# The first four gate blocks of a Fourier mixer computed from rows that are not yet normalised, and a reordered last head before them

## The reference

```python
def rms_norm(x, g):
    var = jnp.mean(xf * xf, axis=-1, keepdims=True)
    return (xf * lax.rsqrt(var + EPS)) * g

# layer 1, after x = x + gate * (y @ w_out)
h = rms_norm(x, norm_g[1]) * (1.0 + sc) + sh
def fourier_mixer(h, w_in, w_out):
    u, z = jnp.split(h @ w_in, 2, axis=-1)      # 2048 features each
    y = jnp.fft.fft2(ug, axes=(1, 3), norm='ortho').real
    return (y * jax.nn.silu(z)) @ w_out
```

## Time and profile before

| what | us |
|---|---|
| median of three executions | 2534.68 |
| the profiled execution's own time | 2534.45 |
| its span | 2532.8 |
| TensorE (PE) busy | 2466.3 |
| VectorE (DVE) busy | 1632.1 |
| ScalarE (ACT) busy | 993.6 |
| mean granted TensorE clock, as a share of full speed | 0.989 |

### The profile page before, as it was taken

The page is one execution under the profiler, slowest core; times in us unless marked ns, Lnnn a source line. Parts: engine busy times, 40 slices in busy tenths (PEclk is TensorE's granted clock), DMA queues, the critical chain, the costliest instruction groups (busy, mean ns, idle before and its releaser), DMA issues.

```text
span 2532.8 us, 40390 instructions
## 1 busy us (share of the span) xinstructions
PE 2466.3 (97%) x14398; PEld 2151.2 (85%) x14398; DVE 1632.1 (64%) x2378; ACT 993.6 (39%) x1338; POOL 118.1 (5%) x138
## 2 busy tenths in 40 slices
PE   7999999999999998999999999989999999999998
PEld 3888888888888876888889999989999878888886
DVE  7577777777777765445555343468999985534446
ACT  4345444444444423333345222234555543322223
POOL 0011111121111100000000000000000000000000
PEclk9999999999999998999999999999999999999999
DMA  6212222222212222222222222222232222222223
GB/s 242 80 58 76 81 66 66 69 71 75 74 58 75 100 84 75 83 84 75 87 89 91 86 88 91 91 92 89 93 99 99 92 85 99 91 99 91 93 98 100
DMA packets 61983, 223.90 MB, mean 88 GB/s; under 512 B 6736, under 2 KB 8784, under 8 KB 61552
## 3 DMA queue, kind: packets, MB, share of 16 engines
q1 hardware_dynamic: 58992, 211.08, 25.1%
q0 software_dynamic: 2944, 12.19, 1.4%
HBM read 221.15 MB, written 2.10 MB: 88 GB/s over the span
## 4 chain that ended last, share of the span: by engine, by line
PE 92%; DVE 4%; ACT 1%; issue 1%; DMA 1%; ACTq 0%; DVEq 0%; SPq 0%
PE ps L489 81%; PE ps L662 4%; PE ps L684 1%; PE ps L546 1%; PE ps L675 1%; DMA ada_raw<-in_ada_weights_dram 1%; DVE w_lo L1593 1%; PE ps L694 1%; PE ps L695 1%; ACT w_hi L1050 1%; PE ps L696 1%; PE ps L703 1%; PE ps L649 1%; DVE n_tmp L1617 0%; PE ps L632 0%
## 5 line engine op out<-in xcount | busy, mean ns | idle before, releaser
L1050 ACT ACTIVATE w_hi<-w_raw 128x1024 fp32r<-128x1024 f32 (+1 forms) x360 | 377.8, 1050 | 935.7 <-PE ps L489 925.9
L1593 DVE TENSOR_TENSOR w_lo<-w_raw,w_hi 128x1024 fp32r<-128x1024 f32 (+1 forms) x360 | 435.3, 1209 | 226.4 <-ACT w_hi L1050 224.3
L489 PE MATMUL ps<-n_hi,w_hi 128*128 128x512 f32 (+1 forms) x992 | 320.3, 354 | 12.2 <-DVE n_lo L1620 8.5
L489 PE MATMUL ps<-n_lo,w_hi 128*128 128x512 f32 (+1 forms) x992 | 319.4, 354 | 0.0
L489 PE MATMUL ps<-n_hi,w_lo 128*128 128x512 f32 (+1 forms) x992 | 318.0, 352 | 0.0
L489 PE MATMUL ps<-h_hi,w_hi 128*128 128x512 f32 x640 | 266.6, 417 | 4.3 <-DVE h_lo L1725 2.6
L489 PE MATMUL ps<-h_hi,w_lo 128*128 128x512 f32 x640 | 251.8, 393 | 0.0
L489 PE MATMUL ps<-h_lo,w_hi 128*128 128x512 f32 x640 | 251.0, 392 | 0.0
L489 PEld LDWEIGHTS ps<-n_hi,w_hi 128*128 128x128 f32 x992 | 174.5, 189 | 45.6 <-issue 10.8
L489 PEld LDWEIGHTS ps<-n_lo,w_hi 128*128 128x128 f32 x992 | 174.3, 189 | 26.1 <-issue 0.2
L489 PEld LDWEIGHTS ps<-n_hi,w_lo 128*128 128x128 f32 x992 | 174.5, 189 | 25.8
(11 more groups left out here) (367 smaller groups left out, 4969.1 us busy)
## 6 DMA issues: line engine op xcount, KB each, us to landing
w_raw<-in_weights_dram SPq DMA_DIRECT2D x376, 512.0 KB, 3.3
ada_raw<-in_ada_weights_dram SPq DMA_DIRECT2D x4, 2048.0 KB, 20.9
gate_raw<-in_gate_weights_dram POOLq DMA_DIRECT2D x16, 512.0 KB, 3.6
x<-in_x_dram SPq DMA_DIRECT2D x1, 2048.0 KB, 12.6
x<-in_x_dram POOLq DMA_DIRECT2D x1, 2048.0 KB, 8.0
out_dram<-fin SPq DMA_DIRECT2D x16, 128.0 KB, 1.9
xc<-in_ctx_dram SPq DMA_DIRECT2D x1, 1024.0 KB, 19.3
masks<-in_masks_dram POOLq DMA_DIRECT2D x1, 512.0 KB, 5.1
```

Source lines behind the costliest of these rows:

```text
L489: last = nc.tensor.matmul(o, w, xp, start=start and n == 0, stop=stop and n == 2)
L1050: run(w_hi[:, s, 0:n], w_raw[:, s, 0:n], ACT.Copy).then_inc(hi_ready[s], 1)
L1593: tt(w_lo[:, s, 0:n], w_raw[:, s, 0:n], w_hi[:, s, 0:n].bitcast(F32), ALU.subtract).then_inc(lo_ready[s], 1)
```

## The change

**In the last head.** TensorE's part k of the output projection (k under 4) waits only for the accumulator that was last read from its own bank. On VectorE `passed(2)` stands directly behind `passed(1)`, and `early_after(6)` stands behind the whole norm of head 15's output; on ScalarE the root comes ahead of `early_after(6)`. The zeroing of the sums, the gain `scale[:, 2]` and twice the shift move up here as well.

**On the residual's rows.** As soon as a row of `x` is added, ScalarE writes `g_hi` = x times gain, rounded, and VectorE writes `g_lo`, its remainder (`raw_row`, `raw_row_lo`). TensorE waits for one early row instead of three. The loop over rows 4 to 7 is written out.

**The gates.** Gate blocks 0 to 3 (`RAW`) multiply these rows (`raw_gate`), with the mean for the norm placed inside the first. Beside each of the 8 triples stand two matmuls of 2 columns with the same weights and the shift (`shift_hl`: hi and lo). VectorE multiplies each result by the rate and adds up the shift's part (`raw_gate_scaled`), ScalarE applies the Silu with that as its bias (`raw_gate_row`). The normalised rows are made between these steps (`normal_tmp`, `normal_hi`, `normal_lo`), since the other 12 gate blocks and the transform still use them. Only gate block 4 is woven with their arrival. The remaining 11 blocks are spread as one beside each of rows 0 to 4 of the transform and two beside each of rows 5 to 7.

```diff
@@ pe_head, begin_output
-                        pe.wait_ge(acc_free, HEADS * 6 + 2)
+                        if k < EARLY:
+                            pe.wait_ge(acc_free, HEADS * 6 - 1 + k)
@@ TensorE, rows 4 to 7 and the gates
-            residual(RC, (KD - EARLY) // 2, 2, whole(y_hi, y_lo), T, done=EARLY)
-            mean(N1, T, n1["sum"][:, 0])
+            for i in range((KD - EARLY) // 2):
+                st.enter(0, 4)
+                for a in range(2):
+                    for q in range(2):
+                        s = take(a * 2 + q)
+                        if q == 0:
+                            pe.wait_ge(RC["res"], (3, 5, 7, 8)[i * 2 + a])
...
+            def raw_gate(n):
+                s = take(n % 2)
+                if n == 0:
+                    pe.wait_ge(RC["res"], KD + 1)
+                if n > 1:
+                    pe.wait_ge(z_scaled, n - 1)
+                side = ps[:, (4, 3, 5, 7)[n], 0:2]
+                for k in range(KD):
+                    if n == 0:
+                        if k == KD - 2:
+                            mean(N1, T, n1["sum"][:, 0])
+                        pe.wait_ge(raw_lo, k + 1)
+                    c = slice(k * P, (k + 1) * P)
+                    done = tiles(s, [ps[:, n % 2]], whole(g_hi, g_lo), [k], k == 0, k == KD - 1, k)
...
+                    nc.tensor.matmul(side, w_hi[:, s, c], shift_hl[:, k], start=k == 0, stop=False)
+                    done = nc.tensor.matmul(side, w_lo[:, s, c], shift_hl[:, k], start=False, stop=k == KD - 1)
...
+            s = take(0)
+            pe.wait_ge(z_out, RAW + 1)
+            tiles(s, [ps[:, 0]], as_cut(N1, whole(nf_hi, nf_lo)), range(KD), True, True).then_inc(w_used[s], 1)
+            turn(0)
+            gates_of(RAW // 2, 1)
+            over_tokens(0)
@@ ScalarE, rows
+            def raw_row(m_):
+                act.wait_ge(RC["res"], m_ + 3)
+                run(g_hi[:, m_], x1[:, m_], ACT.Identity, bias=zero[:], scale=scale[:, 2, m_:m_ + 1]).then_inc(raw_hi, 1)
+                act.wait_ge(RC["add"], m_ + 2)
+                run(n1["sq"][:, 0], x1[:, m_], ACT.Square).then_inc(RC["sq"], 1)
             for k in range(EARLY):
-                square_one(RC, k, x1[:, k], n1["sq"][:, 0], 2)
+                raw_row(k)
@@ ScalarE, normalised rows
+            after(0); raw_gate_row(0); normal_hi(0); after(1); raw_gate_row(1); normal_hi(1); normal_hi(2)
+            after(0); raw_gate_row(2); normal_hi(3) ... normal_hi(6); after(1); raw_gate_row(3); normal_hi(7)
@@ VectorE, last head
                 passed(1)
+                if i is None:
+                    mine(10)
+                    passed(2)
                 cut_output()
                 take_z()
                 early_after(5)
-                mine(10)
-                passed(2)
-                early_after(6)
@@ VectorE, early rows
+            def early_row(k):
+                dve.wait_ge(early_done, k + 1)
+                stt(x1[:, k], ps[:, k], gates[:, k, 0:1], x1[:, k], ALU.mult, ALU.add).then_inc(RC["res"], 1)
+                raw_row_lo(k)
+                add_square(RC, k, *sums)
+            early_row(0); early_row(1); after(2 * EARLY - 1); early_row(2); early_row(3)
@@ VectorE, gates and normalised rows
+            def raw_gate_scaled(n):
+                side = ps[:, (4, 3, 5, 7)[n]]
+                st.wait_done(dve, n % 2)
+                own.mark(v.tensor_copy(z_part[:, n:n + 1], side[:, 0:1]))
+                tt(z_rows[:, n], ps[:, n % 2], rate, ALU.mult)
+                own.wait()
+                tt(z_shift[:, n:n + 1], z_part[:, n:n + 1], side[:, 1:2], ALU.add).then_inc(z_scaled, 1)
+            after(0); raw_gate_scaled(0); normal_tmp(0); normal_tmp(1); normal_lo(0)
+            after(1); raw_gate_scaled(1); normal_lo(1); normal_tmp(2); normal_tmp(3); normal_lo(2)
+            after(0); raw_gate_scaled(2); normal_lo(3)
+            for k in range(4, KD - 1):
+                normal_tmp(k)
+                normal_lo(k)
+            after(1); raw_gate_scaled(3); normal_tmp(KD - 1); normal_lo(KD - 1)
```

More of the change, by code:

```diff
@@ L54 @@
 EARLY = 4
+RAW = 4
 Z_BANK = 2
@@ L326, in program @@
         N0, N0C, N1, NMIX = [norm_sems(t, "sum", "mean", "root", "tmp", "hi", "lo") for t in ("n0", "n0c", "n1", "nmix")]
[L327 to L328 removed]
+        NFIN, NOUT = norm_sems("nfin", "mean", "root"), norm_sems("nout", "sum", "mean", "root", "lo")
+        NF1, NF2 = [norm_sems(t, "mean", "root", "hi", "lo") for t in ("nf1", "nf2")]
         R0, R0C, RC, RF, RD1, RM, RD2 = [
@@ new lines, in _ @@
+            for i in range(RAW // 2):
+                st.enter(0, 2)
+                raw_gate(2 * i)
+                raw_gate(2 * i + 1)
+                st.leave(1)
+            st.enter(0, 2)
+            s = take(0)
[4 more added lines that the diff above has]
+            over_tokens(0)
+            st.leave(1)
+            with hinted(pe, 0, 2) as a:
+                st.enter(a, 2)
+                turn(a * 2 + 1)
+                gates_of(a + 3, 0)
+                over_tokens(a * 2 + 1)
+                turn(a * 2 + 2)
+                gates_of(a + 3, 1)
+                over_tokens(a * 2 + 2)
@@ L810, in pe_group @@
+            st.leave(2)
+            with hinted(pe, 0, 3) as b:
+                st.enter(b, 2)
+                turn(b + 5)
+                gates_of(b + 5, 0)
+                over_tokens(b + 5)
+                gates_of(b + 5, 1)
+            st.leave(3)
             def pe_group(i, j):
@@ new lines, in _, with normal_tmp, normal_lo @@
+            rate = n1["sq"][:, 0]
+            dve.wait_ge(N1["root"], 1)
+            own.link(v.reciprocal(rate, rate))
+            def normal_tmp(k):
+                if k > 1:
+                    dve.wait_ge(N1["lo"], k - 1)
+                stt(n1["tmp"][:, k % 2], x1[:, k], scale[:, 2, k:k + 1], rate, ALU.mult, ALU.mult
+                    ).then_inc(N1["tmp"], 1)
+            def normal_lo(k):
+                dve.wait_ge(N1["hi"], k + 1)
+                stt(nf_lo[:, k], n1["tmp"][:, k % 2], ada1[:, k, 0:1], nf_hi[:, k].bitcast(F32), ALU.add, ALU.subtract
+                    ).then_inc(N1["lo"], 1)
@@ new lines, in _ @@
+            normal_tmp(1)
+            normal_lo(0)
+            after(1)
+            raw_gate_scaled(1)
+            normal_lo(1)
+            normal_tmp(2)
+            normal_tmp(3)
+            normal_lo(2)
+            st.leave(1)
+            st.enter(0, 2)
+            after(0)
+            raw_gate_scaled(2)
+            normal_lo(3)
+            for k in range(4, KD - 1):
+                normal_tmp(k)
+                normal_lo(k)
+            after(1)
+            raw_gate_scaled(3)
@@ L1984, in fold @@
+            normal_tmp(KD - 1)
+            normal_lo(KD - 1)
+            st.leave(1)
             def fold(c, later=0):
@@ L2014, in frequencies_lo @@
                 tt(lo[:, 0:HALF_T + 1], p_cos[:], hi[:, 0:HALF_T + 1], ALU.subtract).then_inc(dve_ft, 1)
+            fold(0)
+            for n in range(2):
+                own.link(v.memset(middle[:, n:HALF_T + 1:2], (-1) ** n / T ** 0.5))
             st.enter(0, 2)
             after(0)
-            fold(0)
+            turned_lo(0)
+            fold(0, 1)
             dve.wait_ge(dft_split["act"], 1)
```

214 lines of the change are left out of this document (133 added, 81 removed).

## The result

| | median us | runs | lowest to highest |
|---|---|---|---|
| before, same chip | 2534.18 | 20 | 2531.92 to 2537.18 |
| after | 2537.62 | 20 | 2535.61 to 2541.32 |

The ratio is 1.0015, with a 95% interval of 1.0009 to 1.0022: 3.4 us slower. Forecast were 2525.0 and a range up to 2533. The profiled execution after took 2541.32 us, its span is 2539.6. It is the longest of the 20, 3.7 us above their median, so what the change costs in all is read from the medians; the trace serves for places and durations.

The account below looks back on a forecast made before the run. TensorE, 92% of the span, was taken as the bound, so gains come only from its waits and low clock. The last head's entry gave 4.1 us, the later steps 5.6, in all 9.7: 2525.0 us, range 2521 to 2533.

Parts of the forecast that it names:

- Memory adds nothing: In the sum: each slot's load follows its split as before, DMA share of the transform 0.26, so no time added.
- the clock: Rival, raw gates: tiny matmuls lower TensorE's clock, a block takes 12 us instead of 7.15; 2539.5 us, chance 0.08.
- A: Entering the last head: the counter wait causes TensorE's gap at 868.83 to 871.41; removing it saves 4.1 us.
- Fetch: Rival: the gap at 871.41 is instruction fetch at a loop exit, so nothing is saved there; 2529.1 us, chance 0.25.
- B: Last head's states: two updates move up from 918.11, the 2.2 us wait and low clock go; lead 4.0 us.
- D: First output block needs the first early row, not the third: no wait; lead 7.5, then 9.2 us after two blocks.
- C: Last head's norm: root earlier, reciprocal no longer behind block 8's split; y_lo at 929.2 instead of 934.0, lead 4.8 us.
- E: Output rows: raw rows take 2.9 us each, so block 10 waits 3.3 us plus 1.5 low clock; lead falls to 4.4.
- F: Gates ahead of the norm: two-column matmuls cost 0.11 us apiece, 7.15 a block; late normalised rows put the fold at 1021.3.
- G: Transform: 11 blocks instead of 14 remain, 75.4 us, no wait; stretch ends at 1097.3 instead of 1102.9.
- the dear pairs: Rival: two-column matmuls cost 0.25 us each, 6.7 us later; 2531.7 us, chance 0.14 shared with late blocks 11, 13, 15.

Follow-up runs that it names:

- after256: The changed kernel with 160 unused bytes behind shift2, so all later tiles lie 256 bytes above their place before: 2525.01 us (0.9967).
- acc_only: The kernel before with only TensorE's counter waits of the early blocks taken one by one: 2529.93 us (0.9984).
- lasthead: The kernel before with those counter waits one by one, passed(2) moved up on VectorE and the root ahead of early_after(6) on ScalarE: 2526.59 us (0.9971).
- supply: The kernel before with 56 more two-column matmuls behind the mean of N1, where TensorE waits for the norm: 2547.03 us (1.0052).
- fewside256: The changed kernel with tiles 256 bytes up, leaving out 28 of the 32 pairs of two-column matmuls: 2524.76 us (0.9964).

## Why the prediction was wrong

**The failed step is a term that the sum did not have.** The unit in it, "one takes 0.228 and a block of 24 takes 5.45 us", was taken from before and held fixed. The sentence "Memory adds nothing" in the sum spoke of the loads of weights; of the tiles' places nothing was said. The diff showed the two tiles taken ahead of `z_rows`; the prediction did not ask what they push. That term measures 12.1 to 12.6 us (after256 against the changed kernel), more than the whole forecast gain, and turned its sign; the range missed by 4.6 us. No rival had it. The one on the slower side was the clock; its 2539.5 lies near the measured 2537.6 by chance, for in the raw gates of the changed kernel the clock stayed up (the stretch's view):

```profile
984.00:1009.00 25.00, 25.00 (x134) 20.89 (x133) 16.12 (x21) 10.97 (x14) 0.00 (x0) 1.00 0.20 64
```

**The rest of the sum held until the transform.** In after256, where the unit holds, the last loop head's norm stands 0.6 us later than before (868.34 against 867.71), which I add to the leads:

| place | forecast lead, A included | after256 |
|---|---|---|
| kept rows, 934.05 before | 4.1 + 4.8 = 8.9 | 8.0 + 0.6 = 8.6 |
| end of the output rows, 984.84 | 4.1 + 4.4 = 8.5 | 7.65 + 0.6 = 8.3 |
| first transposes, forecast 1021.3 - 4.1 | at 1017.2 | 1018.1 - 0.6 = 1017.5 |
| first products behind the transform, 1119.10 | 9.7 | 6.0 + 0.6 = 6.6 |

- **A** was right in cause and size: 3.7 us by the medians, 4.1 in the trace (acc_only starts 1.2 later and is 3.0 ahead at the first products behind the transform), forecast 4.1. The Fetch rival was wrong for 871. For 1445 it was right that a gap may go where no wait was changed; its cause is not shown.
- **B to D** were right together: in after256 no wait on `states` is left, the reciprocal stands right behind the root, block 8 starts unwaited at 928.91 (11.2 us ahead with the 0.6, forecast 11.6), and TensorE wants block 10 at 942.86 - 2.88 - 0.6 = 939.4, forecast 942.95 - 4.1 = 938.9. lasthead against acc_only prices B and ScalarE's half of C: 3.3 us by medians, 4.7 in the trace (1116.14 to 1111.42 at the first products behind the transform). D has no run of its own.
- **E** was right in place and nearly in size, 2.6 to 2.9 for 3.3 us, but it bought less than it seemed: moved away, it returns at block 11, so the cover of 0.9 us a block was too thin for one more row.
- **F** was right in the unit. A triple with its pair took 0.93 us in the changed kernel (984.71 to 985.64), 0.91 in after256, forecast 0.9. The rule of the Trainium skill, "TensorE: Matmul & The Clock Gate", section "Back-to-back issue gap", some 25 ns for a matmul of 1 to 64 columns, does not fit: 0.233 us for two (0.913 less three times 0.227). The same section gives that figure for an isolated matmul and says that it counts too little where weights are loaded between small ones, as they are here. Of the waits forecast at 0.9, 3.9 and 0.5 the first two came, with 0.5 and 3.4.
- **G** failed by some 3 us: "so no wait". Two things were missed. The low clock behind the 3.4 us wait lasts into the first block of the transform (from 1018.13 it is 7.5 us to the first products with `F_hi`, before 6.0; the clock is 0.80 from 1018.1 to 1026), where I had allowed 0.6. And TensorE waits 1.3 for `t_lo`, because ScalarE stands still 2.5 us in front of `t_hi` in the code that was written out anew. TensorE and ScalarE in after256:

```profile
1016.36 1.22 PE L494 MATMUL ps<-y_lo,w_hi 128*128 128x512 f32 x2 [3.38 <-DVE y_lo L2106]
1018.13 1.12 PE L778 MATMUL ps<-ident,h_fold 128*128 128x128 f32 x4
...
1034.39 0.39 PE L494 MATMUL ps<-F_hi,t_hi 128*128 128x258 f32 x1 [1.26 <-DVE t_lo L2164]
```

```profile
1033.02 0.60 ACT L1391 ACTIVATE t_hi<-ps 128x512 fp32r<-128x512 f32 x1 [2.53 <-issue]
```

So after256 meets 2525.0 partly by luck: the 3 us lost in G came back as the 2.6 us of the gap at 1445. Against lasthead all the rest of the change (D, VectorE's half of C and the raw gates) is 1.7 us slower at the end of the transform (1113.13 against 1111.42); by the medians it is 1.6 faster at the end of the run, which is no more than the gap at 1445 and less than these runs can tell apart. So the raw gates bring nothing that is shown, and what is shown of the gain is in the last head.

Two slips in the sums change nothing: the 6.7 us of the dear pairs are 48 matmuls (24 pairs) x 0.14, and 2524.9 + 4.1 is 2529.0.

## What to carry to other kernels

Where a change takes memory, list which tiles it pushes and by how many bytes, and compare the mean duration of an untouched group of matmuls before reading any wait. In a kernel like this one, try the rows that TensorE streams at a multiple of 256 bytes from its weights, by padding or by the order of the allocations: it cost nothing here and was worth more than the reordering. A lead gained at one place is only kept where the next wait, here VectorE's rows and a split, does not follow right behind it.

## What was not expected of the hardware

- Matmuls with 512 float32 columns were slower at each distance of rows and weights that was run and is no multiple of 256 bytes: `mg` 389 ns at 0 and at 256, 397 at 64 (`g` only 390 to 393), 399/394/392 (by product) at 96, 395 at 128; the whole kernel +4.4, +16.4 and +12.0 us. The 264-column matmuls on `xg` took 285 to 286 ns in the kernel before and 283 to 286 in the changed one. They are no test of this, for their rows lie 2112 bytes apart and so at several distances in both. The Trainium skill, "SBUF — State Buffer", section "Operand start alignment", allows any multiple of the element's size and says that this is about legality, not speed; these runs add the speed for one form.
- Gaps of 2.3 to 3.2 us that the trace ties to nothing come and go while nothing is changed at their place: on TensorE at 1445 us in all ten kernels run without the raw gates except supply, and in none with them; at 1646 in fewside256; on ScalarE in the transform of the changed kernel (2.4 to 2.7 us in all its variants). The Trainium skill, "Runtime: NRT & Kernel Launch", section "Instruction fetch mechanics", says that a taken branch out of the fetched pages stops the sequencer for a DMA; supply, where 56 matmuls ahead take the gap at 1445 away, agrees with it, but no run here shows the fetch itself.
- 112 passes of two columns in a row, behind an idle time of 2.3 us, ran at a granted clock of 0.50 (1.2 GHz) from first to last, 0.213 us each, and held TensorE for 23.9 us; two passes among three matmuls of 512 columns left it at 1.00 and took 0.117 each. So a row of tiny matmuls was no cheap filler for this wait.
